# Playing the latents' first norm and input projection in 29 steps between the prompt tile's stages

## The chip, the cores and the metric

The kernel runs on one core of one Trainium2 chip. The metric is the device time of one launch in microseconds (us). A core has TensorE (PE in the profile; its weight loads are PEld), VectorE (DVE), ScalarE (ACT), GpSimd (POOL) and SyncE (SP), which run side by side and wait for each other on semaphores only. A "q" behind an engine's name is its sequencer, which also issues DMAs. Here SP issues every ordinary load and store, and POOL every gather.

## The reference, cut to what matters

There are five tiles of 128 tokens, all of width 1024 and float32: one prompt tile (tile 0) and four latent tiles (tiles 1 to 4). Both groups go through two layers:

```python
for li in range(2):
    h = rms_norm(x, n1) * (1 + scale1) + shift1
    out = mixer_ab(h, ...) if li == 0 else attention(h, ...)   # mixer_ab begins with h @ w_in, 1024 x 2080
    x = x + g1 * out
    x = x + g2 * peer(rms_norm(x, n2) * (1 + scale2) + shift2, wq, keys, u, v)
```

`peer` picks 128 of 16,384 experts for each token (8 heads, 16 each), takes the dot product of the token's row h with each expert's row of u, puts it through gelu and the gate, and sums the experts' rows of v with these weights. In layer 0 the prompt and the latents depend on each other in nothing. Their shift, scale and gate differ.

## The kernel before

**Experts.** A *slot* is one expert of every token of a tile: an indirect DMA that brings 128 rows of 2048 floats (u beside v, 1 MB) into one of eight places of a ring in SBUF (`Experts.ring`). There are 10 tile visits (2 layers, 5 tiles) of 128 slots, 1280 in all. POOL issues the gathers in order (`gather_all`): it waits until the tile's experts are selected (`selected`) and until the place is free (`used`). DVE then forms the dot (`dot`, L1437), ACT applies gelu (L1458) and gate (L1461), and the weighted v row is added either by DVE (`add_row`, L1446) or by PE, which multiplies by a diagonal made on ACT (L1464) and sums in PSUM (`sum_rows`, L1472). Which engine adds a slot is set for each stage by a list of ring places (`PE_0` to `PE_8`: none to all eight on PE).

**Stages.** All other work is written as stages (norm, in, decay, gla, pool, out, norm, query, select), each of which ends at a meeting of SP, ACT, DVE and PE (`meet`, L150 to L165). POOL takes no part in the meetings. A stage has units, and after each unit every engine calls `tick`, which plays slots in line until a running goal is reached: the stage's start, plus a lead, plus rate times units. The tables `FIRST_RATES` and `REST_RATES` hold rate, places on PE and lead by stage. Slots beyond `limit` (`allow`) aren't played.

**Order in layer 0.** Modulation, load, then the prompt's stages, in which no slots are played since none is selected (`NO_ROWS`). Then `load_gate(0, 0)`, which loads the row g2 between two meetings. Then for the four latent tiles: norm (`norm_stage`) and in (`projection_stage`, five chunks of 416 columns of `l0_w_in`, four tiles each, 20 units), decay, then gla, pool, out, norm, query and select of tile 1 alone. Tile 0's slots are played beside all these. `finish(0)` plays what is left of them, the gate of the latents is loaded, and then gla and pool of tiles 2 to 4, and their out, norm, query and selects, are done with tile 1's slots beside them.

By the rates and units, 53 slots are due by the end of the latents' first norm and in stage, 128 at `finish(0)`, and 255 at the end of tile 2's selection. Layer 1 follows with its own table. The last tiles' slots are played in a loop with nothing beside them.

The lines below are the parts that the diff touches and what calls them.

Of the kernel before, what the change touches and what calls it, by code (L numbers as in the profile page):

```python
# [23 lines left out]
P = 128  # L24
D = 1024
# [104 lines left out]
class Core:  # L130


    def __init__(self, nc, a, block, meeting):
        self.nc, self.a, self.block, self.meeting, self.meetings = nc, a, block, meeting, 0
        self.bg = None
        self.cleared = []

    def meet(self, clear=()):
# [36 lines left out]
class Stage:  # L175
# [10 lines left out]

    def __enter__(self):
        self.stack.__enter__()
        self.base = self.core.bg.goal if self.core.bg else 0
        if self.rate:  # L190
            self.core.bg.on_pe = self.on_pe
            self.core.bg.align(self.base + self.lead)
            self.base = self.core.bg.goal
        return self

    def __exit__(self, kind, *e):
        if kind is None and self.sems:
            if self.core.bg:
                self.core.bg.align(self.base + int(self.units * self.rate))
            self.core.meet(self.sems)  # L200
        return self.stack.__exit__(kind, *e)

    def tick(self, name, eng, unit):
        if self.core.bg and self.rate:
            self.core.bg.upto(name, eng, self.base + int(unit * self.rate))
# [1481 lines left out]

def layer0_rows(core, tag, tiles, pr, rates):  # L1690
# [46 lines left out]
def first_experts(core, tag, tile, layer, rates, w_slots=4):  # L1737

    bg = core.bg
    output_stage(core, f"{tag}_out", [tile], layer, core.env["h"], core.a[f"l{layer}_w_out"], rates["out"], w_slots)  # L1740
    with Stage(core, f"{tag}q") as q:
        qT, keys, keys_in = q.sb("qT", [P, 2 * PH, P]), q.sb("keys", [P, 2 * PH * NKEYS + 2 * TOPK]), q.sem("keys_in")
        queries(core, tag, [tile], layer, qT, keys, keys_in, rates, w_slots)
        select_stage(core, f"{tag}_select", tile, 0, qT, keys, keys_in, bg.experts, bg.gates, rates["select"])


def other_experts(core, tag, tiles, layer, q0, rates):
# [13 lines left out]
PE_0, PE_2, PE_4, PE_6, PE_8 = (places_on_pe(n) for n in (0, 2, 4, 6, 8))  # L1761


PROMPT_RATES = {"norm": (3.0, PE_4, 5), "in": (2.0, PE_0, 4), "qk": (2.5, PE_4, 5), "attend": (1.5, PE_2, 0), "out": (3.0, PE_2, 4),
                "query": (1.2, PE_0, 2), "select": (2.1, PE_8, 3)}
FIRST_RATES = {"norm": (2.0, PE_4, 5), "in": (1.8, PE_0, 4), "decay": (4.0, PE_4, 3), "gla": (1.6, PE_8, 4), "pool": (2.0, PE_2, 4),
               "out": (2.0, PE_0, 4), "query": (0.8, PE_0, 2), "select": (1.5, PE_8, 3)}
REST_RATES = {"norm": (2.0, PE_4, 5), "gla": (1.3, PE_8, 4), "pool": (2.0, PE_2, 4), "out": (2.0, PE_0, 4), "query": (1.6, PE_0, 2),
              "first select": (1.2, PE_8, 3), "select": (2.1, PE_8, 3)}
LATENT_RATES = {"norm": (3.0, PE_4, 5), "in": (2.3, PE_0, 4), "qk": (4.5, PE_4, 5), "attend": (1.5, PE_2, 0), "out": (3.0, PE_0, 4),  # L1770
                "query": (1.5, PE_0, 2), "first select": (2.0, PE_8, 3), "select": (2.1, PE_8, 3)}

# [1 line left out]
def program(nc, a):  # L1774
    prompt, latents = list(range(PROMPT_TILES)), list(range(PROMPT_TILES, TILES))
    first, others = latents[0], latents[1:]
    mods = nc.dram_tensor("mods", (2, 2 * MODW), F32).ap()
    with ExitStack() as outer:
        meeting = outer.enter_context(nc.semaphore("meeting"))
        core = Core(nc, a, outer.enter_context(nc.Block()), meeting)  # L1780
        mem = outer.enter_context(Stage(core, "core"))
        env = core.env = {"mods": mods}
        modulation_stage(core, 0, "mod0")
        core.env.update(x=mem.sb("x", [P, TILES, D]), h=mem.sb("h", [P, TILES, D]), ident=mem.sb("ident", [P, P]))
        load_stage(core)
        bg = Experts(core, mem)
        core.bg = bg
        bg.prepare()
        bg.gather_all()


        with Stage(core, "p0_mix") as m:
            pr, la, st = m.sb("pr", [P, PROMPT_TILES, IN0]), m.sb("la", [P, PROMPT_TILES, 2 * QK]), None
            layer0_rows(core, "p0", prompt, pr, NO_ROWS)
            layer0_decays(core, "p0", prompt, pr, la, st, NO_ROWS)
            layer0_mix(core, "p0", prompt, [0], pr, la, st, NO_ROWS)
        first_experts(core, "p0", 0, 0, NO_ROWS)
        bg.load_gate(0, 0)


        bg.allow(1)
# [48 lines left out]
        bg.finish(q)  # L1850
        bg.tiles(q + 1, 2 * TILES)
        core.meet()
        store_stage(core)
# [68 lines left out]
```

## Time and profile before

| what | value |
|---|---|
| median of 3 runs | 4656.49 us (4644.45 to 4656.57) |
| the profiled execution's own time | 4654.32 us |
| its span, first to last instruction | 4652.5 us |
| gathers | 1280, 1342 MB, 71.5% of the span of the 16 DMA engines |
| direct loads and stores | 228 MB, 12.7% |
| busy | PE 64%, DVE 68%, ACT 31%, POOL 35% |

The span is cut into 40 slices of 116 us below. Each digit is the busy share of a slice in tenths. The first three slices and part of the fourth hold modulation and prompt, and no gather.

```profile
PE   7452955457677876545663656555578477766665
DVE  0127756667569885676967868777769778866766
PEclk9675978778888998768986779767887789988888
DMA  6345968655798999889997999968989899999998
```

### The profile page before, as it was taken

How to read it: one execution, taken by the hardware profiler on the slowest of the kernel's cores; microseconds unless marked ns; L12 is line 12 of the kernel's file. 1: busy time of each engine (PE TensorE's matmuls, PEld its weight loads, DVE VectorE, ACT ScalarE, POOL GpSimd, SP SyncE). 2: the span in 40 equal slices, each digit the busy share in tenths (PEclk: the TensorE clock that was granted, in tenths of full speed). 3: DMA queues.
4: the chain of work that ended last, by engine and by line, in shares of the span. 5: the costliest groups of instructions: out<-in, count | busy, mean ns of one | idle time of the engine just before them, and what ended most of it. 6: DMA issues, size and time to landing. Idle time of an engine off the chain costs nothing.

```text
span 4652.5 us, 33905 instructions
## 1 busy us (share of the span) xinstructions
PE 2974.9 (64%) x9295; PEld 1569.9 (34%) x9295; DVE 3172.1 (68%) x6186; ACT 1445.6 (31%) x4073; POOL 1613.6 (35%) x1284
## 2 busy tenths in 40 slices
PE   7452955457677876545663656555578477766665
PEld 1251533423543321224331442334435353322222
DVE  0127756667569885676967868777769778866766
ACT  0111242124123331162323513243249223333222
POOL 0002323111333444343433324433433344455553
PEclk9675978778888998768986779767887789988888
DMA  6345968655798999889997999968989899999998
GB/s 230 119 154 209 390 258 317 249 194 198 300 365 348 407 409 383 368 338 395 419 376 291 365 367 399 403 268 338 418 349 339 325 389 418 381 422 422 409 422 372
DMA packets 234034, 1572.54 MB, mean 338 GB/s; under 512 B 31716, under 2 KB 35624, under 8 KB 58888
## 3 DMA queue, kind: packets, MB, share of 16 engines
q0 software_dynamic: 184320, 1342.26, 71.5%
q1 hardware_dynamic: 49544, 228.32, 12.7%
q8 instruction: 70, 1.15, 0.1%
q14 instruction: 100, 0.82, 0.0%
HBM read 1567.23 MB, written 3.24 MB: 338 GB/s over the span
## 4 chain that ended last, share of the span: by engine, by line
DMA 36%; DVE 24%; PE 23%; ACT 6%; issue 6%; POOL 2%; DVEq 1%; SPq 1%; PEldq 0%; ACTq 0%; PEld 0%; POOLq 0%
DMA core_ring<-in_l_uv,core_experts 21%; DVE core_ring L1437 6%; PE sum_rows L1472 6%; DVE core_yv L1446 4%; DMA mod_w<-in_l_w_mod 3%; PE mod_ps L311 2%; PE s_in_ps L426 2%; POOL core_ring L1429 2%; PE s0b_query_pq L1225 2%; ACT L1458 1%; DVEq L155 1%; DMA p_in_w<-in_l_w_in 1%; PE s0b_gla_pd L743 1%; PE p_in_ps L426 1%; PE s0b_out_po L497 1%
## 5 line engine op out<-in xcount | busy, mean ns | idle before, releaser
L1429 POOL DMA_INDIRECT core_ring<-in_l_uv,core_experts x1280 | 1613.4, 1260 | 3007.2 <-PE sum_rows L1472 1266.6
L1437 DVE CUSTOM_DVE_ANT_0 core_ring<-core_ring,core_hc 128x1024 f32<-128x1024 f32 x1280 | 1550.5, 1222 | 632.9 <-DMA core_ring<-in_l_uv,core_experts 405.1
L1472 PE MATMUL sum_rows<-core_ring,core_diag 128*128 128x512 f32 x2720 | 1508.8, 699 | 663.6 <-ACT core_diag L1464 515.1
L1472 PEld LDWEIGHTS sum_rows<-core_ring,core_diag 128*128 128x128 f32 x2720 | 557.3, 219 | 1501.9 <-ACT core_diag L1464 837.4
L1458 ACT ACTIVATE core_wt<-core_wt 128x1 f32<-128x1 f32 x1280 | 257.5, 201 | 1844.8 <-DVE core_wt L1437 1733.5
L1446 DVE SCALAR_TENSOR_TENSOR core_yv<-core_ring,core_wt,core_yv 128x1024 f32<-128x1024 f32 x600 | 768.5, 1281 | 43.8 <-ACT core_wt L1461 43.2
L1461 ACT ACTIVATE core_wt<-core_wt,core_gates 128x1 f32<-128x1 f32 x1280 | 376.8, 294 | 64.9
L1464 ACT ACTIVATE core_diag<-core_ident,core_wt 128x128 f32<-128x128 f32 x680 | 273.0, 402 | 22.2
L311 PE MATMUL mod_ps<-mod_w,mod_silu 128*2 128x512 f32 x384 | 184.6, 642 | 69.4 <-DMA mod_w<-in_l_w_mod 69.2
L1458 ACT ACT_TABLE_LOAD x112 | 143.7, 1283 | 51.7 <-SPq L165 38.4
L300 DVE TENSOR_TENSOR mod_m<-mod_m,mod_ps 2x512 f32<-2x512 f32 x24 | 16.2, 674 | 151.5 <-PE mod_ps L311 151.5
L426 PE MATMUL s_in_ps<-s_in_w,s_mixh_hT 128*128 128x416 f32 x320 | 113.8, 519 | 8.0 <-DMA s_in_w<-in_l_w_in 8.0
L311 PEld LDWEIGHTS mod_ps<-mod_w,mod_silu 128*2 128x2 f32 x384 | 32.9, 89 | 220.1 <-issue 166.2
L1437 DVE DVE_READ_ACCUMULATOR2_ANT core_wt<- 128x1 f32 x1280 | 104.5, 82 | 0.0
L1501 PE MATMUL sum_rows<-core_zero 128*128 128x128 f32 x160 | 37.0, 424 | 105.2 <-SPq L165 64.0
L1149 ACT ACT_TABLE_LOAD x72 | 92.4, 1283 | 16.2 <-SPq L165 10.6
L1225 PE MATMUL s0b_query_pq<-s0b_h_hT,s0b_query_w 128*128 128x384 f32 x256 | 86.0, 500 | 5.7 <-DMA s0b_query_w<-in_l_peer_wq 5.7
L1225 PE MATMUL p_query_pq<-p_h_hT,p_query_w 128*128 128x128 f32 x512 | 65.7, 290 | 31.7 <-DMA p_query_w<-in_l_peer_wq 31.6
L426 PEld LDWEIGHTS s_in_ps<-s_in_w,s_mixh_hT 128*128 128x128 f32 x320 | 61.6, 193 | 60.4 <-issue 51.6
L1225 PEld LDWEIGHTS p_query_pq<-p_h_hT,p_query_w 128*128 128x128 f32 x512 | 62.7, 203 | 36.6 <-DMA p_query_w<-in_l_peer_wq 36.1
L1501 PEld LDWEIGHTS sum_rows<-core_zero 128*128 128x128 f32 x160 | 34.4, 327 | 107.4 <-issue 64.4
L1225 PE MATMUL s1c_query_pq<-s1c_h_hT,s1c_query_w 128*128 128x256 f32 x256 | 61.1, 401 | 10.5 <-ACT s1cq_qT L1233 5.6
(736 smaller groups left out, 3164.7 us busy)
## 6 DMA issues: line engine op xcount, KB each, us to landing
mod_w<-in_l_w_mod SPq DMA_DIRECT2D x24, 2048.0 KB, 8.0
core_ring<-in_l_uv,core_experts POOLq DMA_INDIRECT x1280, 12.2
p_query_w<-in_l_peer_wq SPq DMA_DIRECT2D x32, 512.0 KB, 6.9
p_in_w<-in_l_w_in SPq DMA_DIRECT2D x5, 1664.0 KB, 7.3
s_in_w<-in_l_w_in SPq DMA_DIRECT2D x5, 1664.0 KB, 10.8
p_out_w<-in_l_w_out SPq DMA_DIRECT2D x8, 1024.0 KB, 10.6
s0a_query_w<-in_l_peer_wq SPq DMA_DIRECT2D x16, 512.0 KB, 7.6
s0b_query_w<-in_l_peer_wq SPq DMA_DIRECT2D x16, 512.0 KB, 8.3
```

Of the source, the lines that this page charges most:

```text
L311: mm = nc.tensor.matmul(ps[0:2, n % 2, :], act_c[:, k, :], w[:, n % WSLOTS, k, :], start=(k == 0), stop=(k == DK - 1))
L426: mm = nc.tensor.matmul(ps[:, i % 4, 0:chunk], hT[:, k, t * P:(t + 1) * P], w[:, n % 2, k, :], start=(k == 0), stop=(k == DK - 1))
L1149: nc.scalar.activation(sc[:, n % 2, 0:w], sc[:, n % 2, 0:w], ACT.Exp, bias=mx[:, n % 2:n % 2 + 1], accum_out=den[:, t % 2, head:head + 1]) ...
L1225: mm = nc.tensor.matmul(pq[:, n % 2, 0:tok], w[:, n % w_slots, k, :], hT[:, k, :], start=(k == 0), stop=(k == DK - 1))
L1429: nc.gpsimd.indirect_dma_start(self.ring[:, r, :], None, core.a[f"l{layer}_uv"], bass.IndirectOffsetOnAxis(ap=self.experts[:, t, n:n + 1], ...
L1437: nc.vector.tensor_tensor_reduce(self.ring[:, r, 0:D], self.ring[:, r, 0:D], self.hc[:], 1.0, 0.0, ALU.mult, ALU.add, self.wt[:, r:r + 1]) ...
L1446: nc.vector.scalar_tensor_tensor(self.yv[:], self.ring[:, r, D:], self.wt[:, r:r + 1], self.yv[:], ALU.mult, ALU.add).then_inc(self.used[r ...
L1458: nc.scalar.activation(self.wt[:, r:r + 1], self.wt[:, r:r + 1], ACT.Gelu_apprx_tanh).then_inc(self.gelu_done, 1)
L1461: nc.scalar.activation(self.wt[:, r:r + 1], self.wt[:, r:r + 1], ACT.Copy, scale=gate).then_inc(self.wt_done, 1)
L1464: nc.scalar.activation(self.diag[:, r, :], self.core.env["ident"][:], ACT.Copy, scale=self.wt[:, r:r + 1]).then_inc(self.diag_done, 1)
L1472: mm = nc.tensor.matmul(self.py[:, c * 512:(c + 1) * 512], self.diag[:, r, :], self.ring[:, r, D + c * 512:D + (c + 1) * 512], start=False ...
L1501: nc.tensor.matmul(self.py[:, c * P:(c + 1) * P], self.zero[:], self.zero[:], start=(c * P % 512 == 0), stop=False, skip_group_check=True)
```

## The change

`Early` holds the latents' first norm and input projection as 29 steps. PE's share is four groups of eight transposes (steps 3 to 6) and twenty groups of eight matmuls of 416 columns (steps 8 to 27). ACT's is the squares, the root and the evacuations (one step behind PE). DVE's is steps 1 to 5. Its operands lie in the ring and in the row sums' PSUM tile, which are empty until tile 0's experts are selected. Its eight loads (three broadcast rows, five chunks of weights) are issued by POOL ahead of the first gather, and POOL waits for the last evacuation before it gathers. The steps are played by the same `align` and `tick` as slots are, through `core.fill`, beside the prompt's stages by the table `EARLY_RATES`. The latents' norm and in stage is gone. The rates from there to tile 2's selection change, and `finish(0)` with the latents' gate moves behind gla and pool of tiles 2 to 4.

```diff
         bg.prepare()
-        bg.gather_all()
...
-        with Stage(core, "p0_mix") as m:
...
-            layer0_rows(core, "p0", prompt, pr, NO_ROWS)
...
-        first_experts(core, "p0", 0, 0, NO_ROWS)
-        bg.load_gate(0, 0)
...
         with Stage(core, "s0_mix") as m:
             pr = m.sb("pr", [P, LATENT_TILES, IN0])
-            layer0_rows(core, "s0", latents, pr, FIRST_RATES)
+            early = core.fill = Early(core, bg, latents, pr)
+            early.load()
+            bg.gather_all()
+            with Stage(core, "p0_mix") as p:
...
+                layer0_rows(core, "p0", prompt, p_pr, EARLY_RATES)
+                layer0_decays(core, "p0", prompt, p_pr, p_la, None, EARLY_RATES)
+                layer0_mix(core, "p0", prompt, [0], p_pr, p_la, None, EARLY_RATES)
+            first_experts(core, "p0", 0, 0, EARLY_RATES)
+            early.finish()
+            core.fill = bg
+            bg.load_gate(0, 0)
+            bg.allow(1)
             la, st = ...
             layer0_decays(core, "s0", latents, pr, la, st, FIRST_RATES)
             layer0_mix(core, "s0a", latents, [0], pr, la, st, FIRST_RATES)
             first_experts(core, "s0a", first, 0, FIRST_RATES, 3)
+            bg.allow(2)
+            layer0_mix(core, "s0b", latents, [1, 2, 3], pr, la, st, REST_RATES)
             bg.finish(0)
             bg.load_gate(0, 1)
-            bg.allow(2)
-            layer0_mix(core, "s0b", latents, [1, 2, 3], pr, la, st, REST_RATES)
+EARLY_RATES = {"norm": (0.0, None, 1), "in": (1.4, None, 1), "decay": (1.0, None, 1), "gla": (0.75, None, 1), "pool": (0.0, None, 1),
+               "out": (0.0, None, 1), "query": (0.0, None, 0), "select": (0.5, None, 0)}
-FIRST_RATES = {"norm": (2.0, PE_4, 5), "in": (1.8, PE_0, 4), "decay": (4.0, PE_4, 3), "gla": (1.6, PE_8, 4), "pool": (2.0, PE_2, 4),
-               "out": (2.0, PE_0, 4), "query": (0.8, PE_0, 2), "select": (1.5, PE_8, 3)}
-REST_RATES = {"norm": (2.0, PE_4, 5), "gla": (1.3, PE_8, 4), "pool": (2.0, PE_2, 4), "out": (2.0, PE_0, 4), "query": (1.6, PE_0, 2),
-              "first select": (1.2, PE_8, 3), "select": (2.1, PE_8, 3)}
+FIRST_RATES = {"norm": (2.0, PE_4, 5), "decay": (3.0, PE_4, 3), "gla": (1.6, PE_8, 4), "pool": (2.0, PE_2, 4),
+               "out": (2.0, PE_0, 4), "query": (1.0, PE_0, 2), "select": (0.8, PE_8, 3)}
+REST_RATES = {"norm": (3.0, PE_4, 5), "gla": (2.0, PE_8, 4), "pool": (2.0, PE_2, 4), "out": (3.0, PE_0, 4), "query": (2.0, PE_0, 2),
+              "first select": (1.5, PE_8, 3), "select": (2.1, PE_8, 3)}
```

The new class, cut to the loads and PE's steps:

```python
# load(), on POOL
pool.wait_ge(core.meeting, met)
pool.dma_start(self.gain, broadcast_row(a["l0_norm1"])).then_inc(self.rows_in, 16)
...  # scale and shift in the same way
for n in range(5):
    if n >= 2:
        pool.wait_ge(self.mm_done, (n - 1) * len(self.tiles))
    pool.dma_start(self.w[n % 2], a["l0_w_in"][n]).then_inc(self.w_in[n % 2], 16)
pool.wait_ge(self.out_done, 5 * len(self.tiles))
# step(), on PE
if 3 <= n < 7:
    i = n - 3
    eng.wait_ge(self.h_done, i + 1)
    if i:
        eng.wait_ge(self.hT_done, i)
    ...  # eight transposes of h into ps
elif 8 <= n < 28:
    i = n - 8
    ...  # waits for weights, and for the evacuation of step i - 2
    for k in range(DK):
        mm = nc.tensor.matmul(self.ps[:, i % 2 * 512:i % 2 * 512 + self.CH], self.hT[:, k, t * P:(t + 1) * P], w[:, k, :], ...)
```

## Rows read from the trace of the kernel before

**Rows 1.** Timeline rows that mark stage bounds: start us, us, engine, line, operation, idle before.

```profile
397.40 1.07 POOL L1429 DMA_INDIRECT core_ring<-in_l_uv,core_experts  x1 [396.94 <-DVE core_gates L1362]
403.05 0.33 SPq L353 DMA_DIRECT2D s_norm_gain<-in_l_norm  x1
588.78 0.33 SPq L554 DMA_DIRECT2D s_decay_wz<-in_l_w_alpha_f  x1
946.31 0.94 POOL L1429 DMA_INDIRECT core_ring<-in_l_uv,core_experts  x1 [63.01 <-DVE core_gates L1362]
...
960.19 0.33 SPq L1545 DMA_DIRECT2D core_g<-mods  x1
968.66 0.33 SPq L722 DMA_DIRECT2D s0b_gla_wsum<-in_k_level_sums  x1
```

**Rows 2.** Busy time by stretch (from:to, length; POOL's x counts gathers), clock, DMA.

```profile
core 0: us, PE busy (x) PEld busy (x) DVE busy (x) ACT busy (x) POOL busy (x), PEclk, DMA share, GB/s
120.00:136.00 16.00, 1.97 (x8) 1.57 (x8) 4.22 (x6) 3.66 (x5) 0.00 (x0) 0.50 0.32 98
...
201.00:256.00 55.00, 23.84 (x148) 14.88 (x148) 31.39 (x48) 7.36 (x10) 0.00 (x0) 0.69 0.10 37
347.00:398.00 51.00, 3.84 (x32) 3.65 (x32) 44.72 (x218) 1.82 (x3) 0.60 (x1) 0.57 0.00 1
403.00:588.00 185.00, 141.85 (x392) 75.45 (x392) 135.94 (x173) 49.90 (x153) 70.52 (x57) 0.85 0.96 384
...
664.00:741.00 77.00, 55.66 (x225) 26.94 (x225) 51.82 (x82) 28.79 (x62) 17.00 (x16) 0.83 0.67 263
...
968.00:1159.00 191.00, 144.09 (x637) 73.23 (x638) 135.11 (x215) 72.43 (x148) 34.39 (x32) 0.83 0.53 192
1159.00:1272.00 113.00, 79.61 (x328) 61.07 (x327) 64.37 (x83) 19.66 (x64) 33.27 (x27) 0.83 0.74 294
...
1309.00:1407.00 98.00, 89.76 (x265) 51.63 (x264) 63.31 (x80) 19.89 (x71) 35.29 (x29) 0.96 0.98 391
1407.00:1486.00 79.00, 59.18 (x128) 24.54 (x129) 77.68 (x274) 26.27 (x82) 32.38 (x26) 0.83 0.90 350
588.00:1486.00 898.00, 588.28 (x2232) 343.89 (x2233) 601.34 (x1174) 258.82 (x662) 236.49 (x198) 0.80 0.71 277
...
4000.00:4652.00 652.00, 417.53 (x752) 156.12 (x752) 440.84 (x634) 196.20 (x677) 312.34 (x248) 0.85 0.98 407
```

**Rows 3.** The page's costliest groups: a slot's parts (busy, mean ns; idle before).

```profile
L1437 DVE CUSTOM_DVE_ANT_0 core_ring<-core_ring,core_hc 128x1024 f32<-128x1024 f32 x1280 | 1550.5, 1222 | 632.9 <-DMA core_ring<-in_l_uv,core_experts 405.1
L1472 PE MATMUL sum_rows<-core_ring,core_diag 128*128 128x512 f32 x2720 | 1508.8, 699 | 663.6 <-ACT core_diag L1464 515.1
...
L1458 ACT ACTIVATE core_wt<-core_wt 128x1 f32<-128x1 f32 x1280 | 257.5, 201 | 1844.8 <-DVE core_wt L1437 1733.5
L1446 DVE SCALAR_TENSOR_TENSOR core_yv<-core_ring,core_wt,core_yv 128x1024 f32<-128x1024 f32 x600 | 768.5, 1281 | 43.8 <-ACT core_wt L1461 43.2
L1461 ACT ACTIVATE core_wt<-core_wt,core_gates 128x1 f32<-128x1 f32 x1280 | 376.8, 294 | 64.9
L1464 ACT ACTIVATE core_diag<-core_ident,core_wt 128x128 f32<-128x128 f32 x680 | 273.0, 402 | 22.2
```

**Rows 4.** The page's DMA issues: KB each, median us to landing.

```profile
p_in_w<-in_l_w_in SPq DMA_DIRECT2D x5, 1664.0 KB, 7.3
```

**Rows 5.** Timeline of PE in the prompt's in stage.

```profile
165.23 5.85 PE L426 MATMUL p_in_ps<-p_in_w,p_mixh_hT 128*128 128x416 f32 x16 [0.17 <-DMA p_in_w<-in_l_w_in]
```

**Rows 6.** Timeline of PE in the prompt's gla stage, third score batch.

```profile
222.93 1.16 PE L767 MATMUL p_gla_pscore<-p_gla_qe,p_gla_e 64*128 64x128 f32 x16 [2.70 <-DVE p_gla_sc L838]
```

**Rows 7.** Timeline of DVE: the prompt's selection begins; a tile's turn ends.

```profile
351.43 3.26 DVE L1300 MAX8 p_select_vals<-p_select_pscore 128x8 f32<-128x128 f32 x16 [44.41 <-PE p_select_pscore L1274]
...
1507.11 0.91 DVE L1490 MEMSET core_yv<- 128x1024 f32 x1 [0.28 <-DVE core_x L1523]
```

More of the change, by code:

```diff
@@ L134, in __init__ @@
         self.nc, self.a, self.block, self.meeting, self.meetings = nc, a, block, meeting, 0
-        self.bg = None
+        self.bg, self.fill = None, None
         self.cleared = []
@@ L188, in __enter__ @@
         self.stack.__enter__()
-        self.base = self.core.bg.goal if self.core.bg else 0
+        self.base = self.core.fill.goal if self.core.fill else 0
         if self.rate:
-            self.core.bg.on_pe = self.on_pe
-            self.core.bg.align(self.base + self.lead)
-            self.base = self.core.bg.goal
+            self.core.fill.on_pe = self.on_pe
+            self.core.fill.align(self.base + self.lead)
+            self.base = self.core.fill.goal
         return self
@@ L197, in __exit__ @@
         if kind is None and self.sems:
-            if self.core.bg:
-                self.core.bg.align(self.base + int(self.units * self.rate))
+            if self.core.fill:
+                self.core.fill.align(self.base + int(self.units * self.rate))
             self.core.meet(self.sems)
@@ L203, in tick @@
     def tick(self, name, eng, unit):
-        if self.core.bg and self.rate:
-            self.core.bg.upto(name, eng, self.base + int(unit * self.rate))
+        if self.core.fill and self.rate:
+            self.core.fill.upto(name, eng, self.base + int(unit * self.rate))
     def sb(self, name, shape, dt=F32):
@@ L1686, in tiles, with __init__, load, _ @@
         self.goal = self.limit = last * SLOTS
+class Early:
+    STEPS = 29
+    CH = IN0 // 5
+    def __init__(self, core, bg, tiles, pr):
+        nc = core.nc
+        self.core, self.tiles, self.pr, self.goal, self.on_pe = core, tiles, pr, 0, None
+        self.done = {"vector": 0, "scalar": 0, "tensor": 0}
+        flat = bg.ring[:].rearrange("p r n -> p (r n)")
+        size, rows = DK * self.CH, DK * P * len(tiles)
+        self.hT = flat[:, 0:rows].rearrange("p (k n) -> p k n", k=DK)
+        self.w = [flat[:, rows + i * size:rows + (i + 1) * size] for i in range(2)]
+        at = rows + 2 * size
+        self.gain, self.scale, self.shift = (flat[:, at + i * D:at + (i + 1) * D] for i in range(3))
+        self.ss, self.ps = bg.wt[:, 0:len(tiles)], bg.py
+        new = lambda name: nc.alloc_semaphore(f"early_{name}")
+        self.rows_in, self.sq_done, self.mean_done, self.sqrt_done = new("rows_in"), new("sq_done"), new("mean_done"), new("sqrt_done")
+        self.order, self.h_done, self.tr_done, self.hT_done = new("order"), new("h_done"), new("tr_done"), new("hT_done")
+        self.w_in, self.mm_done, self.out_done = [new(f"w_in{i}") for i in range(2)], new("mm_done"), new("out_done")
+    def load(self):
+        core, nc, a = self.core, self.core.nc, self.core.a
+        met = 4 * core.meetings
+        mods, c = core.env["mods"], cond_of(self.tiles)
+        @core.block.gpsimd
+        def _(pool):
+            pool.wait_ge(core.meeting, met)
+            pool.dma_start(self.gain, broadcast_row(a["l0_norm1"])).then_inc(self.rows_in, 16)
+            pool.dma_start(self.scale, broadcast_row(mods[c, D:2 * D])).then_inc(self.rows_in, 16)
+            pool.dma_start(self.shift, broadcast_row(mods[c, 0:D])).then_inc(self.rows_in, 16)
+            for n in range(5):
+                if n >= 2:
+                    pool.wait_ge(self.mm_done, (n - 1) * len(self.tiles))
+                pool.dma_start(self.w[n % 2], a["l0_w_in"][n]).then_inc(self.w_in[n % 2], 16)
+            pool.wait_ge(self.out_done, 5 * len(self.tiles))
+    def step(self, name, eng, n):
+        nc, x, h = self.core.nc, self.core.env["x"], self.core.env["h"]
+        tiles, NT = self.tiles, len(self.tiles)
+        if name == "scalar":
+            if n == 0:
+                for i, t in enumerate(tiles):
+                    nc.scalar.activation(h[:, t, :], x[:, t, :], ACT.Square, accum_out=self.ss[:, i:i + 1]).then_inc(self.sq_done, 1)
+            elif n == 1:
+                eng.wait_ge(self.mean_done, 1)
+                nc.scalar.activation(self.ss, self.ss, ACT.Sqrt).then_inc(self.sqrt_done, 1)
+            elif 4 <= n < 8:
+                i = n - 4
+                eng.wait_ge(self.tr_done, i + 1)
+                nc.scalar.activation(self.hT[:, :, i * P:(i + 1) * P], self.ps[:].rearrange("p (k n) -> p k n", k=DK),
+                                     ACT.Copy).then_inc(self.hT_done, 1)
+            elif n >= 9:
+                i = n - 9
+                c, t = divmod(i, NT)
+                eng.wait_ge(self.mm_done, i + 1)
+                nc.scalar.activation(self.pr[:, t, c * self.CH:(c + 1) * self.CH], self.ps[:, i % 2 * 512:i % 2 * 512 + self.CH],
+                                     ACT.Copy).then_inc(self.out_done, 1)
+        elif name == "vector":
+            order = self.ordered
+            if n == 1:
+                eng.wait_ge(self.rows_in, 48)
+                order(eng, nc.vector.scalar_tensor_tensor(self.scale, self.scale, 1.0, self.gain, ALU.add, ALU.mult))
+                eng.wait_ge(self.sq_done, NT)
+                nc.vector.tensor_scalar(self.ss, self.ss, 1.0 / D, EPS, ALU.mult, ALU.add).then_inc(self.mean_done, 1)
+            elif 2 <= n < 6:
+                i = n - 2
+                if i == 0:
+                    eng.wait_ge(self.sqrt_done, 1)
+                    order(eng, nc.vector.reciprocal(self.ss, self.ss))
+                row = h[:, tiles[i], :]
+                order(eng, nc.vector.scalar_tensor_tensor(row, x[:, tiles[i], :], self.ss[:, i:i + 1], self.scale, ALU.mult, ALU.mult))
+                nc.vector.tensor_tensor(row, row, self.shift, ALU.add).then_inc(self.h_done, 1)
+        else:
+            if 3 <= n < 7:
+                i = n - 3
+                eng.wait_ge(self.h_done, i + 1)
+                if i:
+                    eng.wait_ge(self.hT_done, i)
+                for k in range(DK):
+                    mm = nc.tensor.transpose(self.ps[:, k * P:(k + 1) * P], h[:, tiles[i], k * P:(k + 1) * P], self.core.env["ident"][:])
+                mm.then_inc(self.tr_done, 1)
+            elif 8 <= n < 28:
+                i = n - 8
+                c, t = divmod(i, NT)
+                if t == 0:
+                    eng.wait_ge(self.w_in[c % 2], c // 2 * 16 + 16)
+                if i < 2:
+                    eng.wait_ge(self.hT_done, NT)
+                else:
+                    eng.wait_ge(self.out_done, i - 1)
+                w = self.w[c % 2].rearrange("p (k n) -> p k n", k=DK)
+                for k in range(DK):
+                    mm = nc.tensor.matmul(self.ps[:, i % 2 * 512:i % 2 * 512 + self.CH], self.hT[:, k, t * P:(t + 1) * P], w[:, k, :],
+                                          start=(k == 0), stop=(k == DK - 1))
+                mm.then_inc(self.mm_done, 1)
+    ordered_n = 0
+    def ordered(self, eng, ins):
+        ins.then_inc(self.order, 1)
+        self.ordered_n += 1
+        eng.wait_ge(self.order, self.ordered_n)
+    def upto(self, name, eng, goal):
+        while self.done[name] < min(goal, self.STEPS):
+            self.step(name, eng, self.done[name])
+            self.done[name] += 1
+    def align(self, goal):
+        goal = min(goal, self.STEPS)
+        if goal > self.goal:
+            self.goal = goal
+            for name in self.done:
+                @self.core.bg.engine(name)
+                def _(eng):
+                    self.upto(name, eng, goal)
+    def finish(self):
+        self.align(self.STEPS)
+        core = self.core
+        @core.block.tensor
+        def _(pe):
+            pe.wait_ge(self.out_done, 5 * len(self.tiles))
```

5 lines of the change are left out of this document (1 added, 4 removed).

## The prediction

> **What bounds the kernel now.** I read the busy shares by slice first, then stage bounds on the timeline, then busy time by stretch, then the parts of one slot. No gather can start before 397.40 us, when tile 0's experts are selected [rows 1]. From then on 1280 slots must be played, and the question for each stage is what sets its pace. Where DMA has a share of 0.96 to 0.98, as in the latents' norm and in stage (403 to 588), tile 1's query (828 to 890), the others' query (1309 to 1407) and the last loop (4000 to 4652), it is the DMA engines, at 384 to 407 GB/s. Between 588 and 1486 the share is 0.71 [rows 2]: the stages' own chains of PE, ACT and DVE set the pace there and slots are played too thinly for the DMA. The widest hole is tile 1's selection: POOL stood idle for 63.01 us up to 946.31, since tile 0's slots had run out, and the next stage began only at 968.66 [rows 1]. The prompt's stages have no slots at all, a DMA share of 0.10 in gla and 0.00 in select, and little PE work [rows 2].
>
> **Where the counts stand.** From rates, units and leads: before, 53 slots are due at the end of the latents' in stage and 255 at the end of tile 2's selection (about 1486). After the change, 0 are due when decay starts and again 255 at the end of that selection. All that follows has the same table and the same count. So the change is worth three terms: the stage that goes, the 53 slots that must be played elsewhere, and what the prompt's stages grow by.
>
> **1. The stage that goes.** From its first issue at 403.05 to decay's first at 588.78 [rows 1]: -185.7 us.
>
> **2. The 53 slots, and the moved finish.** Differences by stage, from the tables (units times rate plus lead): decay -4, tile 1's query +4, its select +14 (19 for 5, since the limit of 128 cut it before), gla of tiles 2 to 4 +17, out +6, norm +3, query +7, tile 2's select +6. Sum 53. Their prices:
> - gla. The prompt's took 55 us without slots, of which about 7 are the wait for constants, so 48 for 8 units. Tile 1's took 77 with 16 gathers (8 units), tiles 2 to 4 took 191 with 32 gathers, 36 slots due (24 units) [rows 2]. The first pair gives 22/16 = 1.4 us a slot, the second (191 - 13 - 144)/36 = 0.95. All slots are PE's here, and a denser stage leaves less idle time: I take 1.5, so 25.5 us.
> - select. 51 us without slots, 79 with 26 [rows 2]: about 1.1 to 1.3 a slot, which is the dot's 1.22 us [rows 3], since DVE does nothing but select. 14 at 1.3 is 18. Tile 2's select already has a DMA share of 0.90, so its 6 cost 2.0 each: 12.
> - query. DMA share 0.98 at 391 to 394 GB/s, so 1.05 MB costs 2.68 us: 11 slots, 29.5 us [rows 2].
> - out and norm. DMA share 0.74 from 1159 to 1272 [rows 2], slots mostly on DVE (1.22 + 1.28 [rows 3]), partly under PE's matmuls: 6 at 1.85, 3 at 2.0: 17.
> - decay, -4 at 1.5: -6.
>
> Together +96, or 1.8 a slot. The ends: 0.95 each (all as in the thin gla) is 50, 2.68 each is 142. Moving `finish(0)`: between 946.31 and 968.66 [rows 1], 22.4 us, the last slots drained, tile 0 was ended and the gate loaded. After it the next gla starts at once. The turn of the tile now stands inside gla: three DVE operations of 1.23 and a clear of 0.91 [rows 7], with a wait for PE's last sums about 8. The gate's load between two meetings, 8.5 (960.19 to 968.66 [rows 1]), stands behind pool. -22.4 + 16.5 = -6. Net of part 2: +90.
>
> **3. The prompt's growth.** Eight matmuls of 416 columns took 2.93 us at full clock (16 in 5.85 [rows 5]). At the lower clock twice that, 5.9.
> - Norm. POOL's first five loads (three rows of 512 KB, two chunks of 1.7 MB, 5 MB) run from about 121 beside the prompt's own rows. At 390 GB/s they need 13 us in a stretch of 16 in which the DMA is 0.32 busy [rows 2]. The row loads gate the prompt's DVE: 0 to +7, I take +3.
> - In. DVE's four tiles (2.5 us each), PE's four transposes and ACT's copies follow each other through one PSUM tile, with ACT's copy placed behind the prompt's own evacuation. Following the waits unit by unit, PE's fourth chunk starts 3.7 us late, the fifth 5.5 late, and after it comes the last transpose with its copy: +9 (5 to 15).
> - Decay. Step 8 lies under the wait for its small loads, step 9 under the state's store: +0.5.
> - Gla. Step 10 lies under the constants' load. Of the six others PE has one behind most score batches. The third batch waited 2.70 us for DVE [rows 6]. A step of 2.93 fills the first gap, the next two push the fourth batch and the values: about +3.3 a half, +6.5. At the lower clock +14.
> - Pool, out, norm, query have rate 0: nothing.
> - Select. DVE works alone from 351.43 to 397.40, 46 us [rows 1, 7]. Ten PE steps are 29 us at full clock, hidden. ACT's exponential needs only evacuations that are done by then. The fifth chunk is asked for some 12 us before its use, and a load of this size landed in 7.3 [rows 4].
> - Finish. The last PE step is issued after select's meeting, behind a PE that has been idle for over 10 us. In stretches like that the granted clock is 0.50 (120 to 136 [rows 2]), so 5.9 + 0.5 for the evacuation: +6.5, on the path of POOL's first gather and of the gate's load alike.
>
> Sum +25.5. Bounds 10 (the early loads and in cost little) and 60 (lower clock throughout: in +15, gla +14, select +13, finish, norm +7, and 5 for chunks that come late).
>
> One rule is weighed here. In the stretches with little PE work the granted clock is 0.50 to 0.69, in the projection 0.85 [rows 2]. The Trainium skill ("TensorE: Matmul & The Clock Gate", section "HAM oscillation — how this bites in real kernels") says that PE falls back to the lower clock in gaps and pays for each return. By it the early steps would also keep the prompt's own matmuls at the higher clock; that would take a few us off part 3. By the rows alone I credit nothing.
>
> No trace shows POOL issuing a direct load. The nearest rows are SP's chunk of the same size, 7.3 us, and the gather of 1 MB, issued in 1.07 [rows 1, 4]. I take SP's. The Trainium skill ("DMA: Bandwidth & Descriptors", section "Anatomy of one DMA — SWDGE (gpsimd) path") gives 2.0 us plus bytes over 436 GB/s for this path, which is 5.9 for a chunk, an estimate; it leaves select hidden as well.
>
> **The sum.** -185.7 + 90 + 25.5 = -70. From the profiled execution's 4654.3 (span 4652.5) that is 4584, and from the median of the runs, 2 us above it, 4586.
>
> **The rivals.**
> - *Every added slot costs a full transfer.* 53 at 2.68 is 142: -185.7 + 142 - 6 + 25.5 = -24, 4632. For it: that is what slots cost in both queries and the last loop. Against it: a share of 0.53 in the long gla and of 0.71 over the whole of 588 to 1486 [rows 2]. 20%.
> - *Added slots are nearly free.* At 0.95: -185.7 + 50 - 6 + 25.5 = -116, 4540. For it: 191 us for three tiles of gla beside 55 for one. Against: selects and queries have no free DVE or DMA. 13%.
> - *Added slots are serial, slower than before.* In gla PE, ACT and DVE hand a chain to and fro. If a tick of two slots stands in it whole, each costs dot, gelu, gate, diagonal and two matmuls, 1.22 + 0.20 + 0.29 + 0.40 + 1.40 = 3.5 [rows 3]. Were that so for all 53: 186, net +20, 4676. It turns the sign above (185.7 + 6 - 25.5)/53 = 3.1 us a slot. Against it: 0.95 to 1.4 measured in gla. 8%, with the prompt's upper bound in it.
> - *The early steps don't hide.* At the lower clock select's ten steps are 59 us against 46, and gla and in grow to their bounds: part 3 is 60, the sum -36, 4620. The rule of the clock speaks against it for select, where PE runs on without a gap, and so does the 0.85 of the projection. 9%.
>
> The forecast itself has 50%, with 4555 to 4615 as its own range. The 80% range reaches to the first rival and most of the second: 4545 to 4645. What a measurement can tell from no change is about 0.3%, 14 us. Faster by more: the forecast, the cheap slots, nearly all of the fourth rival and three quarters of the first, 0.85. Within: 0.08. Slower: 0.07.
>
> **What the profile of the changed kernel should show.** No stage named s_norm or s_in. POOL's first gather at 425 to 430, decay's first load at about 429. Ten groups of PE matmuls inside the prompt's select, all before DVE is done. No idle time of 63 us on POOL before tile 1's selection ends, and a DMA share between decay and tile 2's gates of about 0.82 instead of 0.71. That selection over at about 1416 instead of 1486, and from there to the end the same 3166 us within 10. The prediction is wrong if that last part changes, if POOL's loads hold up the prompt by more than 10 us, or if gla of tiles 2 to 4 takes over 235 us.

## The result, and the profile after

The changed kernel takes 4604.46 us (median of 4 runs, 4596.73 to 4610.74), the kernel before 4656.53 on the same terms: ratio 0.9899, 95% interval 0.9876 to 0.9921, so 52 us or 1.1% faster. A second measurement gave 0.9911 (0.9895 to 0.9926). The forecast was 4586. The span of the profiled execution went from 4652.5 to 4594.9.

The same marks on the timeline of the changed kernel (start, us, engine, line, operation, idle before), to be read against [rows 1]:

```profile
444.86 0.33 SPq L1545 DMA_DIRECT2D core_g<-mods  x1
445.45 0.98 POOL L1429 DMA_INDIRECT core_ring<-in_l_uv,core_experts  x1 [46.44 <-issue]
460.45 0.33 SPq L554 DMA_DIRECT2D s_decay_wz<-in_l_w_alpha_f  x1
842.57 0.33 SPq L722 DMA_DIRECT2D s0b_gla_wsum<-in_k_level_sums  x1
1095.85 0.33 SPq L1545 DMA_DIRECT2D core_g<-mods  x1
```

The latents' norm and in stage (185.7 us) is gone, but the first gather starts at 445.45 instead of 397.40, and decay at 460.45 where the norm stage began at 403.05. That is +57 us. The prompt's own first load was issued 2.5 us earlier in this profile (117.89 against 120.39), so counted from that load it is +60. From decay's first load to tile 2's selection it was 893 us and is 962: +69. From there to the end it was 3171 and is 3172. The sum, -185.7 + 57.4 + 69 + 1.5 = -58, is the difference of the spans.

Busy time by stretch in the changed kernel, with the columns of [rows 2]. In order: the prompt's norm, in, decay, gla; its select; what stands behind select; the wait for the first slots; tile 1's select; gla of tiles 2 to 4; the others' query; decay to tile 2's selection; the rest.

```profile
118.00:135.00 17.00, 1.97 (x8) 1.57 (x8) 4.22 (x6) 3.58 (x5) 2.83 (x5) 0.50 0.92 365
135.00:185.00 50.00, 34.51 (x113) 19.34 (x114) 11.94 (x12) 10.93 (x18) 0.00 (x0) 0.89 0.47 178
185.00:212.00 27.00, 20.91 (x66) 12.24 (x65) 2.37 (x6) 7.67 (x11) 0.00 (x0) 0.75 0.06 16
212.00:286.00 74.00, 58.47 (x259) 31.89 (x257) 31.45 (x48) 10.24 (x16) 1.06 (x2) 0.95 0.20 74
...
377.00:427.00 50.00, 49.42 (x164) 28.57 (x165) 44.58 (x218) 5.83 (x11) 0.53 (x1) 1.00 0.10 35
427.00:445.00 18.00, 16.14 (x46) 8.28 (x44) 0.15 (x1) 1.55 (x3) 0.00 (x0) 1.00 0.00 0
445.00:460.00 15.00, 0.00 (x0) 0.00 (x0) 4.82 (x8) 2.68 (x6) 8.64 (x8) 0.53 0.88 340
...
754.00:843.00 89.00, 53.47 (x145) 26.02 (x146) 78.64 (x271) 22.20 (x72) 25.98 (x22) 0.83 0.79 297
843.00:1064.00 221.00, 173.08 (x734) 88.89 (x734) 158.95 (x252) 89.00 (x201) 61.67 (x53) 0.90 0.68 261
...
1234.00:1329.00 95.00, 85.75 (x258) 49.29 (x257) 67.92 (x86) 19.97 (x73) 31.83 (x31) 0.96 1.01 416
...
460.00:1423.00 963.00, 640.08 (x2381) 367.49 (x2382) 680.00 (x1290) 295.68 (x793) 306.98 (x248) 0.84 0.80 314
1423.00:4594.00 3171.00, 2030.41 (x5840) 1037.88 (x5840) 2340.12 (x4548) 1108.06 (x3214) 1307.22 (x1025) 0.83 0.93 377
```

Two things are to be seen. In select PE is busy for 49.4 of 50 us and goes on for 16.1 of the 18 behind it, with DVE idle: the early steps don't hide there. And gla of tiles 2 to 4 takes in 53 gathers where it took 32, for 30 us more.

What a step costs stands in these two rows of PE's timeline in the changed kernel (the second is the last step, behind select's meeting) and in the page's group for all twenty:

```profile
381.25 56.03 PE L1785 MATMUL sum_rows<-core_ring 128*128 128x416 f32 x160
438.01 5.85 PE L1785 MATMUL sum_rows<-core_ring 128*128 128x416 f32 x16 [0.72 <-DVEq L155]
```

```profile
L1785 PE MATMUL sum_rows<-core_ring 128*128 128x416 f32 x320 | 116.6, 523 | 2.6 <-ACTq L150 1.5
```

The code issues 20 x 8 = 160 matmuls, and the page counts 320. Each of these float32 matmuls leaves two records. Sixteen records are one step, so a step is 5.6 to 5.85 us at full clock. [Rows 5] shows the same: 16 records are one chunk of the prompt's projection, eight matmuls by the code.

### The profile page after: what moved, and what is told of

Read it like the earlier page. It is cut to its first block, busy times and chain, and to the rows that moved or that the text cites. A ratio compares the mean times of both kernels' runs of the same rounds, so it can differ in the third digit from the quotient of the medians.

```text
span 4594.9 us, 34096 instructions
## 1 busy us (share of the span) xinstructions
PE 2993.9 (65%) x9415; PEld 1574.8 (34%) x9415; DVE 3135.5 (68%) x6156; ACT 1456.6 (32%) x4101; POOL 1627.5 (35%) x1292
## 3 DMA queue, kind: packets, MB, share of 16 engines
q8 instruction: 71, 1.16, 0.1%
## 4 chain that ended last, share of the span: by engine, by line
DMA 36%; PE 22%; DVE 22%; issue 7%; ACT 6%; POOL 2%; DVEq 2%; SPq 1%; PEld 1%; PEldq 1%; ACTq 0%; POOLq 0%
DMA core_ring<-in_l_uv,core_experts 20%; PE sum_rows L1472 7%; DVE core_ring L1437 6%; DVE core_yv L1446 4%; DMA mod_w<-in_l_w_mod 3%; PE mod_ps L311 2%; POOL core_ring L1429 2%; ACT L1458 1%; DVEq L155 1%; PE sum_rows L1785 1%; PE p_in_ps L426 1%; DMA s0a_query_w<-in_l_peer_wq 1%; PE s0b_out_po L497 1%; DMA p_in_w<-in_l_w_in 1%; PE p_query_pq L1225 1%
## 5 line engine op out<-in xcount | busy, mean ns | idle before, releaser
L1472 PE MATMUL sum_rows<-core_ring,core_diag 128*128 128x512 f32 x2840 | 1554.6, 692 | 636.0 <-ACT core_diag L1464 535.7
L1472 PEld LDWEIGHTS sum_rows<-core_ring,core_diag 128*128 128x128 f32 x2840 | 577.1, 217 | 1505.9 <-ACT core_diag L1464 866.1
L1446 DVE SCALAR_TENSOR_TENSOR core_yv<-core_ring,core_wt,core_yv 128x1024 f32<-128x1024 f32 x570 | 729.8, 1280 | 39.5 <-ACT core_wt L1461 38.0
L1464 ACT ACTIVATE core_diag<-core_ident,core_wt 128x128 f32<-128x128 f32 x710 | 285.1, 402 | 23.1
L1785 PE MATMUL sum_rows<-core_ring 128*128 128x416 f32 x320 | 116.6, 523 | 2.6 <-ACTq L150 1.5
L1785 PEld LDWEIGHTS sum_rows<-core_ring 128*128 128x128 f32 x320 | 60.8, 193 | 53.8 <-issue 53.0
```

Source lines behind the costliest of these rows:

```text
L1446: nc.vector.scalar_tensor_tensor(self.yv[:], self.ring[:, r, D:], self.wt[:, r:r + 1], self.yv[:], ALU.mult, ALU.add).then_inc(self.used[r ...
L1464: nc.scalar.activation(self.diag[:, r, :], self.core.env["ident"][:], ACT.Copy, scale=self.wt[:, r:r + 1]).then_inc(self.diag_done, 1)
L1472: mm = nc.tensor.matmul(self.py[:, c * 512:(c + 1) * 512], self.diag[:, r, :], self.ring[:, r, D + c * 512:D + (c + 1) * 512], start=False ...
L1785: mm = nc.tensor.matmul(self.ps[:, i % 2 * 512:i % 2 * 512 + self.CH], self.hT[:, k, t * P:(t + 1) * P], w[:, k, :], start=(k == 0), stop= ...
```

## The experiments

Theory A was that a step is 5.85 us of PE, twice what was forecast, and the prompt grows by the steps that no wait covers. Its rival B: the prompt waits for POOL's direct loads or for hand-overs between PE and ACT. For the latents' side, theory C was that a slot in these stages costs about half of a transfer, its rival D a full one.

**half_steps**

```diff
-                for k in range(DK):
+                for k in range(DK // 2):
...
-                                          start=(k == 0), stop=(k == DK - 1))
+                                          start=(k == 0), stop=(k == DK // 2 - 1))
```

> The changed kernel with each of the twenty projection steps cut to four of its eight matmuls (half of the contraction is left out, so the projection is not the reference's). Theory A, a step is 5.85 us of PE and not 2.93 (the prediction's size was half of the true one): eleven steps in select and finish shrink from 62 us to 32 and hide under DVE's 46; the prompt's gla falls from 74 us to about 61; decay loses about 5. The first load of the latents' decay moves from 460 to 425 to 430, the time from 4604 to about 4570. Theory B, the prompt waits for POOL's direct loads or for the hand-over PE to ACT and back: the chunks are as large as before and the number of hand-overs is the same, so the decay's first load stays within 10 us of 460.

Measured: 4584.54 us, ratio to before 0.985 (0.9826 to 0.9875), 20 us below the changed kernel. The run leaves out half of the projection's work, so its time is evidence on the price of a step and not a gain. Decay's first load on the timeline, and PE in select, with the last steps:

```profile
432.18 0.33 SPq L554 DMA_DIRECT2D s_decay_wz<-in_l_w_alpha_f  x1
```

```profile
364.13 22.51 PE L1785 MATMUL sum_rows<-core_ring 128*128 128x416 f32 x64
394.36 8.46 PE L1785 MATMUL sum_rows<-core_ring 128*128 128x416 f32 x16 [7.72 <-ACT s_mix_pr L1748]
410.67 5.92 PE L1785 MATMUL sum_rows<-core_ring 128*128 128x416 f32 x8 [7.85 <-DVEq L155]
```

Decay comes 28 us earlier, gla takes 60.0 us instead of 74.6, and the gate's load follows the selection after 7.8 us instead of 18.0. A holds, B falls. With steps of the size that the prediction assumed, its account of the prompt comes out nearly as written: the ten steps hide in select, gla grows over the kernel before by 5.1 us (6.5 forecast), and select with the last step by 6.8 (6.5 forecast). The row also shows a wait that it had denied. PE stood 7.72 us for an evacuation, since ACT's next evacuations stood behind its exponential, which waited 10.69 us for DVE. And the last step ran 5.92 us for eight records, at the lower clock (0.52 granted) after an idle PE.

**no_gla_steps**

```diff
-EARLY_RATES = {..., "gla": (0.75, None, 1), ..., "select": (0.5, None, 0)}
+EARLY_RATES = {..., "gla": (0.0, None, 1), ..., "select": (0.85, None, 0)}
```

> The changed kernel with the early steps' rate 0 in the prompt's gla and 0.85 in its select, so that six steps move from gla to behind select. Theory A (a step is 5.85 us of PE, and gla hides a part of each): gla falls from 74 us back to 55, select and finish grow by 6 x 5.6 = 34, the prompt as a whole grows by about 15 us, time about 4619. Theory B (the hand-overs are what costs): a step costs the same wherever it stands, no change within 5 us.

Measured: 4634.66 us, ratio 0.9953 (0.9937 to 0.9969), 30 us slower than the changed kernel (24 slower than its second measurement), so theory B falls here too. Gla fell to 56.9 us, and the steps ran in one piece behind the prompt's scores, without waiting for a chunk:

```profile
366.69 95.14 PE L1785 MATMUL sum_rows<-core_ring 128*128 128x416 f32 x272
462.55 5.85 PE L1785 MATMUL sum_rows<-core_ring 128*128 128x416 f32 x16 [0.72 <-DVEq L155]
```

Seventeen steps in 95.14 us are 5.6 each. In gla six cost 18 us, 3.0 each; behind select each costs its whole length. The prompt up to the gate's load grew by 22 us (18 against the second profile of the changed kernel), more than the 15 expected.

Two things made a step in gla cheaper than its length. The waits for DVE that it fills are, in the kernel before, 2.70, 0.65 and 1.67 us in the first half of gla and about the same in the second, some 10 us in all. And PE's own matmuls in gla became faster. The value matmuls of this run and of the changed kernel:

```profile
L775 PE MATMUL p_gla_po<-p_mix_pr,p_gla_sc 128*128 128x128 f32 x8 | 2.4, 461 | 3.4 <-DVE p_gla_sc L838 3.4
L775 PE MATMUL p_gla_po<-p_mix_pr,p_gla_sc 128*128 128x128 f32 x8 | 1.2, 274 | 0.0
```

All of the prompt's own matmuls in gla together take 26.9 us here at a granted clock of 0.69, 24.8 in the kernel before, also at 0.69, and 20.5 in the changed kernel at 0.95. Six steps are 35 us; less 10 for the waits and 4 to 6 for the faster matmuls, 19 to 21 are left, against 18 to 20 measured.

**at_once**

```diff
-EARLY_RATES = {..., "in": (1.4, None, 1), "decay": (1.0, None, 1), "gla": (0.75, None, 1), ..., "select": (0.5, None, 0)}
+EARLY_RATES = {..., "in": (0.0, None, 1), "decay": (0.0, None, 1), "gla": (0.0, None, 1), ..., "select": (0.0, None, 0)}
```

> The changed kernel with every early rate at 0: all 29 steps stand behind the prompt's select, ahead of the gate's load. If a projection step is 5.6 to 5.85 us of PE wherever it stands, the twenty are 115 us, and the squares, roots and transposes before them about 20 more, all on the path. The prompt's own stages fall back to their old lengths (in 44, decay 22, gla 55), which gives back about 32 us of growth, and the 18 us of steps behind select are in the 135 already. Decay's first load comes about 85 us later than in the changed kernel, the time is about 4690, slower than the kernel before. If instead the changed kernel's interleaving hid little, the difference would be under 30 us.

Measured: 4697.09 us, ratio 1.009 (1.0073 to 1.0108): slower than the kernel before. From selection to the gate's load it was 137.1 us, with the twenty steps in these:

```profile
420.99 114.01 PE L1785 MATMUL sum_rows<-core_ring 128*128 128x416 f32 x320 [1.21 <-ACT core_ring L1742]
```

Played in one piece, the early work loses 40 us against the kernel before. The interleaving is worth 93 us of time. Decay's first load came 86 us later than in the changed kernel, counted from the prompt's first load (85 expected).

**spread**

```diff
-"pool": (0.0, None, 1), "out": (0.0, None, 1)
+"pool": (0.01, None, 1), "out": (0.01, None, 1)
-            first_experts(core, "p0", 0, 0, EARLY_RATES)
+            first_experts(core, "p0", 0, 0, dict(EARLY_RATES, norm=(0.01, None, 2)))
```

> The changed kernel with one early step at the start of the prompt's pool, one at the start of its out and two at the start of its second norm, where PE waits 15 to 18 us for constants, weights and DVE; select keeps seven, and none is left behind its meeting. Theory A: the four steps hide, PE is done with the steps in select at 381 + 41 = 422 us, before DVE's 427, and the first gather follows the selection at once instead of 18 us behind it: decay's first load at about 441 instead of 460, time about 4586. If the four steps don't hide (they delay ACT's or PE's own first work of these stages), 0 to 6 us of this are lost for each.

> The kernel spread again: its selection of tile 2 came 14.5 us earlier than the changed kernel's, its median only 5.6. If the stretch behind that selection varies from run to run by some 10 us, the two medians differ by 8 to 15 us this time; if the earlier start costs something later, by 6 or less.

Measured: 4598.86 us (0.9882, 0.9857 to 0.9906), and again, beside the changed kernel's second measurement on the same chip, 4588.78 (0.9862, 0.9842 to 0.9882) against 4610.38. The second pair's intervals don't overlap. POOL's first gather follows the selection at once:

```profile
432.05 0.98 POOL L1429 DMA_INDIRECT core_ring<-in_l_uv,core_experts  x1 [93.55 <-DVE core_gates L1362]
432.83 0.33 SPq L1545 DMA_DIRECT2D core_g<-mods  x1
...
446.94 0.33 SPq L554 DMA_DIRECT2D s_decay_wz<-in_l_w_alpha_f  x1
```

Pool, out and norm took 54.2 us together against 54.3, so four steps cost nothing there. They weren't all hidden under a wait, though. Pool became 2.2 us shorter, out 2.7 longer and norm 0.6 shorter. In the changed kernel PE waits 17.73 us in pool and 15.50 in norm, but only 3.16 for out's weights. What paid for most of the rest is the clock. Behind an early step each of pool's two groups of matmuls took 1.16 us instead of 2.08, at a granted clock of 1.00 instead of 0.50, and out's large group 14.08 instead of 15.84. Pool's first group, in the changed kernel and then in spread:

```profile
294.75 2.08 PE L897 MATMUL p_pool_pd<-p_pool_band,p_mix_pr 128*128 128x128 f32 x8 [17.73 <-DMA p_pool_psc<-in_l_pool_scale]
299.51 1.16 PE L897 MATMUL p_pool_pd<-p_pool_band,p_mix_pr 128*128 128x128 f32 x8 [1.32 <-DMA p_pool_psc<-in_l_pool_scale]
```

Counted from the prompt's first load, tile 2's selection came 14.5 us earlier in the first pair and 19 in the second. The gains in time, 6 and 22 us, lie on both sides. The stretch behind that selection was 3172 us in both profiles of the changed kernel and 3183 and 3179 in these two; over all nine profiles of kernels that are equal there it lies between 3172 and 3184. Why it differs by some 10 us is open.

**old_rates**

```diff
-FIRST_RATES = {..., "decay": (3.0, PE_4, 3), ..., "query": (1.0, PE_0, 2), "select": (0.8, PE_8, 3)}
+FIRST_RATES = {..., "decay": (4.0, PE_4, 3), ..., "query": (0.8, PE_0, 2), "select": (1.5, PE_8, 3)}
-REST_RATES = {"norm": (3.0, PE_4, 5), "gla": (2.0, PE_8, 4), ..., "out": (3.0, PE_0, 4), "query": (2.0, PE_0, 2),
-              "first select": (1.5, PE_8, 3), ...}
+REST_RATES = {"norm": (2.0, PE_4, 5), "gla": (1.3, PE_8, 4), ..., "out": (2.0, PE_0, 4), "query": (1.6, PE_0, 2),
+              "first select": (1.2, PE_8, 3), ...}
```

> The changed kernel with the slot rates of the kernel before from decay on. By the tables 231 slots are due at the end of tile 2's selection instead of 255, and the 24 that are missing are made up later, at the latest in the loops with a DMA share of 0.98, at 2.65 us each. Theory C, a slot in these stages costs about 1.3 to 1.8 us: 24 x (2.65 - 1.4) = 30 us slower than the changed kernel, 4634. Theory D, a slot costs a full transfer wherever it is played: no change, 4604.

Measured: 4626.70 us, ratio 0.9941 (0.9923 to 0.9959), 22 us slower than the changed kernel. Decay to about tile 2's selection, and the rest:

```profile
466.00:1400.00 934.00, 639.91 (x2361) 364.48 (x2362) 630.70 (x1224) 282.92 (x742) 272.68 (x225) 0.83 0.76 299
1400.00:4623.00 3223.00, 2072.88 (x5896) 1054.86 (x5895) 2378.54 (x4603) 1124.99 (x3274) 1333.12 (x1048) 0.82 0.94 378
```

With 24 slots fewer the selection came 28 us earlier, counted from the prompt's first load (36 against the changed kernel's second profile), so a slot costs 1.2 to 1.5 us there. The rest took 52 us longer than in the changed kernel's profile, 2.2 a slot; against the 3184 us that kernels with the new rates also showed it is 40, 1.7 a slot. C holds and D, which expected no change, falls: a slot costs 0.2 to 1 us less in these stages than later. 22 of the changed kernel's 52 us hang on the new rates, or 16 of 43 by its second measurement.

**order_only**

```diff
-            bg.finish(0)
-            bg.load_gate(0, 1)
             bg.allow(2)
             layer0_mix(core, "s0b", latents, [1, 2, 3], pr, la, st, REST_RATES)
+            bg.finish(0)
+            bg.load_gate(0, 1)
```

> The kernel before with one edit: the finish of tile 0 and the latents' gate stand behind gla and pool of tiles 2 to 4, rates as before. The prediction priced this at -6 us (-22.4 for the drain and the gate's load, +8 for the turn inside gla, +8.5 for the gate behind pool): 4650. If the moved finish is where the whole change earns its time, this alone is 20 us or more faster.

Measured: 4644.29 us, ratio 0.9975 (0.9963 to 0.9988), 12 us faster (6 to 17). The sign and the order of size are right. The next gla began 0.8 us after tile 1's selection instead of 22.9, gla grew by 6.3, and out, now behind the gate's load, took 75.5 instead of 84.0, which wasn't expected. Part of what was won by tile 2's selection, 22 us, is missing behind it, where the rest took 3185.

**old_order**

```diff
-            bg.allow(2)
-            layer0_mix(core, "s0b", latents, [1, 2, 3], pr, la, st, REST_RATES)
             bg.finish(0)
             bg.load_gate(0, 1)
+            bg.allow(2)
+            layer0_mix(core, "s0b", latents, [1, 2, 3], pr, la, st, REST_RATES)
```

> The changed kernel with finish and gate back in front of gla of tiles 2 to 4. By the tables 89 slots of tile 0 are played when finish comes, so 39 are played in a loop with nothing beside them, at 2.66 us: 104 us more there, minus the turn inside gla (8). Tile 1's 128 slots then fill the stages up to the others' query and none is left for tile 2's select, where 38 fewer at 1.2 give back 46. Time about 4604 + 50 = 4654, no gain over the kernel before.

Measured: 4668.99 us, ratio 1.003 (1.0019 to 1.004): slower than the changed kernel by 64 us and slightly slower than the kernel before. Tile 1's select to the next gla, in two parts, the second with the drain (the playing of what is left of tile 0's slots):

```profile
762.00:846.00 84.00, 47.99 (x140) 23.27 (x140) 75.22 (x264) 19.98 (x65) 22.79 (x21) 0.83 0.81 307
846.00:963.00 117.00, 71.13 (x140) 27.79 (x140) 69.56 (x100) 33.08 (x115) 50.76 (x43) 0.85 0.96 394
```

The 39 slots with nothing beside them took 109 us up to the gate's load (104 expected). The early projection leaves tile 0 short of stages; without the moved finish, that drain takes its whole gain back. The two edits belong together.

**lead0**

```diff
-"decay": (3.0, PE_4, 3)
+"decay": (3.75, PE_4, 0)
```

> The changed kernel with only the latents' decay at lead 0 and rate 3.75. Of the 11.5 us between the meeting behind the gate and the decay's first load, three slots on DVE make about 10; without them ahead, decay's loads go out at once and the slots are played inside the stage. Expected: first load 10 us earlier, decay's stage longer by half of it, time 4 to 6 us below the changed kernel. If the slots only move, no difference.

> The changed kernel itself, beside the two below on the same chip, so that differences of 5 to 15 us can be told. Its profile should again show the decay's first load about 342 us behind the prompt's first, and 3172 to 3183 us from tile 2's selection to the end. Time about 4604.

Measured: 4606.90 us, ratio 0.9902 (0.9885 to 0.992), beside 4610.38 (0.9911) for the changed kernel: no difference that can be told. From the first gather to decay's first load it was 4.6 us instead of 14.8, decay itself 80.9 instead of 74.8. The three slots moved.

**spread_lead0**, the combination: spread, lead0, and the early rate in gla 0.63 instead of 0.75.

> The kernel of the run named spread with two more edits: one early step moved from the prompt's gla to its select, which has room for eight (45 us of 46), and the latents' decay with lead 0 and rate 3.75 (15 slots as before), so that its loads don't wait behind three slots on DVE. Gla gives 3.3 us, decay's loads start 5 to 6 us earlier. If the lead's three slots only move into the stage, half of that comes back. Decay's end about 6 us earlier than in spread, time 4590.

Measured: 4586.60 us, ratio 0.9846 (0.9833 to 0.9859), the lowest time of a kernel that does all the work: 70 us below the kernel before and 18 below the changed one, whose interval (0.9876 to 0.9921) lies above it. From spread's second measurement (0.9842 to 0.9882) it can't be told apart. The prompt's gla took 68.9 us with one step less, and the gate's load followed the selection after 1.4 us, so nothing waited for PE.

## Why the prediction was right or wrong

- *What bounds the kernel, and the three terms.* Right. The rest behind tile 2's selection was 3171 and 3172 us. That the two agree to 1.5 us is in part luck, since other kernels that are equal there showed up to 3184.
- *Part 1, -185.7.* Right.
- *Part 2, +90.* Measured +69. The forecast price of 1.8 us a slot was too high: (69 + 6)/53 is 1.4, and old_rates gives 1.2 to 1.5. The mis-sized terms are the others' query and tile 2's select, 31 together forecast for 13 slots and 17 measured (172 to 189 us), and out, 11 forecast and 0 measured (84.0 and 83.9 us). The full transfer of 2.68 was charged where the DMA share was 0.98 before. The query stretch after it moved 416 GB/s against 391, so that share was not yet its end. Gla with the turn, 33.5 forecast, was 31 (36 in the second profile). The drain's end, -22.4, was right to 4 us.
- *Part 3, +25.5.* Measured +57, and this is the step that failed: "Eight matmuls of 416 columns took 2.93 us at full clock (16 in 5.85 [rows 5])." They took 5.85. The x16 of [rows 5] counts records, two for each float32 matmul. All that followed was halved: gla +19.7 instead of +6.5, decay +4.7 instead of +0.5, and "Ten PE steps are 29 us at full clock, hidden" were 56. With the last step 18 us stand behind select, where 6.5 were forecast. half_steps shows it: with steps of the assumed size 28 of these us are gone. In and norm, +9 and +3 forecast, were +6.5 and +1.7. Select with the last step grew by 16.8, and what stands behind the gate's load by 10.5 (next point). All six sum to 59.9, and the start that lay 2.5 us earlier makes 57 of it.
- Missed in part 3: decay's loads wait for a clear on DVE that stands behind the lead's three slots, the first of them waiting for its row. From the gate's load to the stage's first issue it was 15.6 us instead of 5.1. Before, this filling of the ring lay inside the norm stage. lead0 shows that it can be moved; a saving by it can't be told.
- *POOL's direct loads.* Right to take them as no dearer than SP's: in no_gla_steps seventeen steps ran without waiting for one. The first five brought the DMA share of the prompt's norm to 0.92 and cost 1.7 us. The three later chunks of the changed kernel took 7.1 to 7.2 us from issue to landing, like SP's 7.3. The Trainium skill ("DMA: Bandwidth & Descriptors", section "Anatomy of one DMA — SWDGE (gpsimd) path") had given 5.9 us for a chunk by its fit, an estimate. The trace shows about 1.2 us more; by either figure nothing waits in select, and nothing did.
- *The clock.* The granted clock in the prompt's gla rose from 0.69 to 0.95 with the steps in it. The prediction credited nothing for that. The prompt's own matmuls there took 20.5 us instead of 24.8, so about 4 us of PE's time, of the size of the "few us" that the prediction weighed. How much of it lies on the path isn't shown on its own, since no run holds the steps and not their clock.
- *The rivals.* Full transfer and serial slots were wrong by old_rates. The serial rival's own price was also too low, by the same reading of records: L1472 has 2720 records for 680 slots [rows 3], four a slot and not two, so a slot's matmuls keep PE busy for 2.2 us and not 1.40. The rival that the early steps don't hide, 4620, was closest to what the prompt did. It has nearly the same price per step, but for another reason: it supposed the lower clock, and the clock was 1.00 in select.
- *Its own signs.* Held: the DMA share between decay and tile 2's gates (0.80, 0.82 forecast), that selection's end (1423 for 1416) and the rest behind it. Missed: POOL's first gather (445 for 425 to 430), decay's first load (460 for 429), and the ten groups of PE matmuls that were all to end before DVE.
- That the time fell inside the forecast's own range (4555 to 4615) is luck. Part 3's error alone would have given 4618. Two errors had opposite signs, +32 in part 3 and -21 in part 2, and the rest was 1.5 longer: 12.5 together, by which the profiled execution, 4596.7, missed its forecast of 4584. The median of the runs lies 8 us above that execution, where it had lain 2 above it before.

## What to carry to other kernels

Before a count in a profile is used as a price, divide it by the instructions that the code issues in that stretch: 320 records for 160 float32 matmuls. Work moved into idle time costs what is longer than the wait that it is put in, so place it by the waits' lengths: four steps were free in three stages that held two waits of over 15 us and a low clock, cost half in gla, where the waits are 1 to 3 us, and cost all behind select. Look at the granted clock around it too: the prompt's own matmuls ran faster with the early steps between them. When slots are played later than before, look where the tile's last ones are played out: the moved finish was worth 12 us alone and 64 together with the early projection.

## What the runs showed of the hardware

A DMA share of 0.98 was not yet the most bytes that the engines moved: the same stretch (the others' query) went from 391 to 416 GB/s and the share to 1.01 with 31 gathers in 95 us instead of 29 in 98. A float32 matmul of 128x416 left two records and took about 0.70 us at full clock (160 of them in 20 steps of 5.6 us). DMAs that POOL issued for 1.7 MB took 0.53 us of its time each (five in 2.7 us), a gather of 1 MB 0.94 to 1.68, 1.27 on average. The same eight records of the prompt's pool (128x128, float32) took 2.08 us at a granted clock of 0.50, after 17.73 us in which PE was idle, and 1.16 at 1.00, when an early step had run up to 1.32 us before them.
